# One reduction for the two norms between the blocks, the meta tokens normed early, the residual's norm on Pool

## The reference

```python
    x = ... two layers ...
    x = rms_norm(x, final_norm)                    # the residual of the second block
    h_res = concatenate([meta_tokens, x])          # 16 + 256 tokens
    h = _rmsnorm(h_res, norm_w_2)                  # what the projections read
    proj = h @ w_in_2
    ...
    return (h_res + concatenate([y_mla, y_na]) @ w_out_2)[:, 16:]
```

## Time and profile before

| | us |
|---|---|
| median of 3 runs | 1233.51 |
| the profiled execution | 1232.0 |
| its span, first to last instruction | 1230.2 |
| PE busy | 1188.6 (97%) |
| DVE busy | 815.4 (66%) |
| ACT busy | 656.6 (53%) |
| POOL busy | 165.7 (13%) |

### The profile page before, as it was taken

One profiled execution on the slowest core, in us unless ns is written; L12 is line 12 of the kernel. 1 busy time (PEld: TensorE's weight loads), 2 busy tenths in 40 slices (PEclk: granted clock), 3 DMA queues, 4 the chain that ended last, 5 costly groups with the idle time before them and its releaser, 6 DMA issues.

```text
span 1230.2 us, 27307 instructions
## 1 busy us (share of the span) xinstructions
PE 1188.6 (97%) x10002; PEld 1147.1 (93%) x10002; DVE 815.4 (66%) x1390; ACT 656.6 (53%) x1121; POOL 165.7 (13%) x228
## 2 busy tenths in 40 slices
PE   6999999999999999999999999999998989998998
PEld 6999999799999999999999899999997887998888
DVE  6767664877777665777665877777656666555764
ACT  5555543656555544555544645555545666656652
POOL 3000000351000000000000450000000000401960
PEclk9999999999999999999999999999997999999999
DMA  7655754445566744556744446556642440544542
GB/s 280 207 190 191 252 169 136 139 155 190 190 200 204 233 160 139 189 200 205 235 162 137 138 155 198 195 188 223 216 158 69 137 131 8 172 155 136 174 154 87
DMA packets 56742, 210.91 MB, mean 171 GB/s; under 512 B 7200, under 2 KB 9280, under 8 KB 56544
## 3 DMA queue, kind: packets, MB, share of 16 engines
q1 hardware_dynamic: 54048, 203.45, 50.1%
q0 software_dynamic: 2480, 6.48, 1.8%
q10 hardware_dynamic: 144, 0.06, 0.0%
HBM read 208.91 MB, written 1.05 MB: 171 GB/s over the span
## 4 chain that ended last, share of the span: by engine, by line
PE 84%; DVE 7%; ACT 3%; issue 3%; POOL 2%; DMA 0%; DVEq 0%; ACTq 0%; SPq 0%
PE bank L1173 25%; PE bank L1174 25%; PE bank L1175 25%; DVE w_lo L748 3%; PE bank L1211 2%; PE bank L1521 2%; PE bank L1501 1%; DVE h_lo L767 1%; ACT w_hi L457 1%; PE bank L1486 1%; DVE probs L886 1%; PE bank L1423 1%; PE bank L1425 1%; PE bank L1424 1%; PE bank L1481 1%
## 5 line engine op out<-in xcount | busy, mean ns | idle before, releaser
L1173 PE MATMUL bank<-h_hi,w_hi 128*128 128x256 f32 (+1 forms) x1992 | 563.4, 283 | 16.9 <-DVE w_lo L748 11.7
L1174 PE MATMUL bank<-h_lo,w_hi 128*128 128x256 f32 (+1 forms) x1992 | 554.3, 278 | 0.0
L1175 PE MATMUL bank<-h_hi,w_lo 128*128 128x256 f32 (+1 forms) x1992 | 554.2, 278 | 0.0
L748 DVE TENSOR_TENSOR w_lo<-w_raw,w_hi 128x1024 fp32r<-128x1024 f32 (+1 forms) x360 | 466.9, 1301 | 73.5 <-ACT w_hi L457 73.2
L457 ACT ACTIVATE w_hi<-w_raw 128x1024 fp32r<-128x1024 f32 (+1 forms) x360 | 397.4, 1108 | 74.4 <-PE bank L1175 56.3
L1173 PEld LDWEIGHTS bank<-h_hi,w_hi 128*128 128x128 f32 x1992 | 377.1, 189 | 24.0 <-issue 19.5
L1174 PEld LDWEIGHTS bank<-h_lo,w_hi 128*128 128x128 f32 x1992 | 377.1, 189 | 0.9
L1175 PEld LDWEIGHTS bank<-h_hi,w_lo 128*128 128x128 f32 x1992 | 376.8, 189 | 0.0
L1173 PE MATMUL bank<-g_hi,w_hi 128*128 128x256 f32 x832 | 230.8, 277 | 1.5 <-DVE g_lo L893 0.8
L1175 PE MATMUL bank<-g_hi,w_lo 128*128 128x256 f32 x832 | 230.0, 276 | 0.0
L1174 PE MATMUL bank<-g_lo,w_hi 128*128 128x256 f32 x832 | 230.0, 276 | 0.0
(11 more groups left out here) (152 smaller groups left out, 1158.6 us busy)
## 6 DMA issues: line engine op xcount, KB each, us to landing
w_raw<-in_w SPq DMA_DIRECT2D x296, 512.0 KB, 3.3
w_raw<-in_wd SPq DMA_DIRECT2D x64, 704.0 KB, 4.1
w_raw<-in_relbias POOLq DMA_DIRECT2D x64, 64.0 KB, 2.3
btab_sb<-in_btab POOLq DMA_DIRECT2D x1, 1536.0 KB, 9.5
x_res<-in_xT SPq DMA_DIRECT2D x2, 512.0 KB, 5.0
out_T<-x_res SPq DMA_DIRECT2D x8, 128.0 KB, 1.7
rope_sb<-in_rope POOLq DMA_DIRECT2D x1, 272.0 KB, 3.6
mats_sb<-in_mats POOLq DMA_DIRECT2D x1, 192.0 KB, 4.0
```

The source lines that it names most:

```text
L748: dve.tensor_tensor(wlo[:, slot, at:at + cols], raw[:, slot, 0:cols], whi[:, slot, at:at + cols].bitcast(F32), ALU.subtract).then_inc(lo_r ...
L1173: pe.matmul(o, h, xh, start=first, stop=False)
L1174: pe.matmul(o, h, xl, start=False, stop=False)
L1175: return pe.matmul(o, lo, xh, start=False, stop=last)
```

## The change

Of the final norm and the norm behind it only one reduction stays on the way to the projections. With s = sum of x² and s6 = sum of x² * (final_gain² + 1e-6), the second norm of the first norm's output is x * (final_gain * norm_w_2) * rsqrt(s6 / 1024 + 1e-12). So:

- Pool computes the gains once (`final_gains`), and in `dn2` of layer 1 adds the squares twice: plain into `acc`, weighted into `wacc` (one more multiplication and one more addition a tile).
- PE makes four sums in place of `sum_norm(6)` (`final_sums`): weighted into one bank, plain into another. The weighted one comes out first.
- ACT makes one `rstd` from the weighted sum, then the eight `h_hi`; only behind these the Ln and Exp of the plain sum, to `rs6`.
- DVE makes `h_32` at once from x by the merged gain, 256 columns wide. The three small gain multiplications and the reduction that stood between the norms now stand ahead of them.
- Pool multiplies x by `rs6` and by the gain (8 tiles, two instructions each), in place of DVE's L972; the first addition to x in `fill` waits for it.
- The meta tokens' norm is made in the first layer: Pool squares and adds (`meta_squares`, 8 x 16 columns) ahead of the convolution, PE sums 16 columns in `conv` at i == 1, ACT makes Ln and Exp at i == 2 (both in each layer, since PE, ACT and DVE loop over the layers), Pool multiplies (`meta_normed`) behind the convolution. ACT and DVE split these 8 x 16 columns at the boundary, ahead of the `rstd` (`hm_hi`, `hm_lo`).

```diff
+        g67, w6 = fin[:, 0:KT], fin[:, KT:2 * KT]
+        wacc, wsq, w6_last = s_all[:, 0:T], s_all[:, T:2 * T], pr_all[:, 0:P]
+        rs6 = rel_all[:, 0:T]
+        xm = x[:, :, T:TM]
+        msq, hm = (h32[:, i, 0:KT * META].rearrange("p (k c) -> p k c", k=KT) for i in (3, 2))
+        hm_hi, hm_lo = (a[:].rearrange("p (k c) -> p k c", k=KT)[:, :, T:TM] for a in (hhi, hlo))
...
-            def add_squares(q, n=T, tiles=range(KT - 1)):
-                for i, k in enumerate(tiles):
+            def add_squares(q, weighted=False):
+                for k in range(KT - 1):
                     pool.wait_ge(sq_done[k % 2], q * 4 + k // 2 + 1)
+                    if weighted:
+                        dst = wsq if k else wacc
+                        if k:
+                            pool.wait_ge(wsq_step, 2 * k - 1)
+                        pool.tensor_scalar(dst, sq[:, k % 2, 0:T], w6[:, k:k + 1], None, ALU.mult).then_inc(wsq_step, 1)
                     if k == 0:
-                        pool.tensor_copy(acc[:, 0:n], sq[:, 0, 0:n]).then_inc(acc_step, 1)
+                        pool.tensor_copy(acc[:, 0:T], sq[:, 0, 0:T]).then_inc(acc_step, 1)
                     else:
-                        pool.wait_ge(acc_step, q * 7 + i)
-                        pool.tensor_tensor(acc[:, 0:n], acc[:, 0:n], sq[:, k % 2, 0:n], ALU.add)\
+                        pool.wait_ge(acc_step, q * 7 + k)
+                        pool.tensor_tensor(acc[:, 0:T], acc[:, 0:T], sq[:, k % 2, 0:T], ALU.add)\
                             .then_inc(acc_step, 1)
+                    if weighted and k:
+                        pool.wait_ge(wsq_step, 2 * k)
+                        pool.tensor_tensor(wacc, wacc, wsq, ALU.add).then_inc(wsq_step, 1)
+
+            def final_gains():
+                pool.tensor_tensor(g67, sml[:, 6 * KT:7 * KT], sml[:, 7 * KT:8 * KT], ALU.mult)
+                pool.tensor_tensor(w6, sml[:, 6 * KT:7 * KT], sml[:, 6 * KT:7 * KT], ALU.mult).then_inc(fin_set, 1)
+                pool.wait_ge(fin_set, 1)
+                pool.tensor_scalar(w6, w6, EPS, None, ALU.add).then_inc(fin_set, 1)
+                pool.wait_ge(fin_set, 2)
+
+            def meta_squares():
+                pool.wait_ge(c_loaded, C_LOADS)
+                pool.tensor_tensor(msq, xm, xm, ALU.mult).then_inc(msq_step, 1)
+                for n, w in enumerate((4, 2, 1)):
+                    pool.wait_ge(msq_step, n + 1)
+                    pool.tensor_tensor(msq[:, 0:w], msq[:, 0:w], msq[:, w:2 * w], ALU.add).then_inc(msq_step, 1)
+
+            def meta_normed():
+                pool.wait_ge(ms_done, 1)
+                pool.tensor_tensor(hm, xm, rs[:, 0, T:TM].unsqueeze(1).broadcast_to([P, KT, META]), ALU.mult)\
+                    .then_inc(hm_step, 1)
+                pool.wait_ge(hm_step, 1)
+                pool.tensor_tensor(hm, hm, sml[:, 7 * KT:8 * KT].unsqueeze(2).broadcast_to([P, KT, META]), ALU.mult)\
+                    .then_inc(hm_step, 1)
...
+            final_gains()
             for l in range(LAYERS):
                 add_squares(3 * l + 1)
+                if l == 0:
+                    meta_squares()
...
                     pool.tensor_tensor(ya[:], ya[:], rs[:, 0, 0:T], ALU.mult).then_inc(y_step, 1)
+                if l == 0:
+                    meta_normed()
                 add_squares(3 * l + 2)
-                add_squares(3 * l + 3)
-            add_squares(7, TM, range(0, KT, 2))
+                if l == LAYERS - 1:
+                    pool.tensor_copy(w6_last, w6[:, KT - 1:KT].broadcast_to([P, P])).then_inc(w6_set, 1)
+                add_squares(3 * l + 3, l == LAYERS - 1)
+            pool.wait_ge(rstd_done, 8)
+            for k in range(KT):
+                pool.tensor_tensor(x[:, k, 0:T], x[:, k, 0:T], rs6, ALU.mult)\
+                    .then_inc(fx_step, 1)
+                pool.wait_ge(fx_step, k + 1)
+                pool.tensor_scalar(x[:, k, 0:T], x[:, k, 0:T], sml[:, 6 * KT + k:6 * KT + k + 1], None, ALU.mult)\
+                    .then_inc(fx_done, 1)
             pool.wait_ge(fx_done, KT)
...
-            def norm(q, n=T):
-
-                act.wait_ge(sum_done, q + 1)
-                rstd(bank[SUM][:, 0:n], 0, D, n, q + 1)
+            def final_norm():
+
+                act.wait_ge(hm_step, 2)
+                act.activation(hm_hi, hm, ACT.Copy).then_inc(hm_hi_done, 1)
+                act.wait_ge(wsum_done, 1)
+                act.activation(lnv[:, 0, 0:T], bank[SUM][:, 0:T], ACT.Ln, scale=1.0 / D, bias=EPS * EPS)\
+                   .then_inc(ln_done, 1)
+                act.wait_ge(ln_done, 7)
+                act.activation(rs[:, 0, 0:T], lnv[:, 0, 0:T], ACT.Exp, scale=-0.5).then_inc(rstd_done, 1)
                 for k in range(KT):
-                    act.wait_ge(h32_done, q * KT + k + 1)
-                    act.activation(hhi[:, k * HS:k * HS + n], h32[:, k % 4, 0:n], ACT.Copy).then_inc(h_hi, 1)
+                    high(7, k, k % 4)
+                act.wait_ge(xsum_done, 1)
+                act.activation(lnv[:, 0, 0:T], bank[XSUM][:, 0:T], ACT.Ln, scale=1.0 / D, bias=EPS)\
+                   .then_inc(ln_done, 1)
+                act.wait_ge(ln_done, 8)
+                act.activation(rs6, lnv[:, 0, 0:T], ACT.Exp, scale=-0.5).then_inc(rstd_done, 1)
...
                     if i == 2:
                         act.wait_ge(vt_done, l + 1)
+                        act.activation(lnv[:, 0, T:TM], bank[OUT][:, T:TM], ACT.Ln, scale=1.0 / D, bias=EPS)\
+                           .then_inc(ms_ln, 1)
                         act.activation(v32[:].rearrange("p t c -> p (t c)"), bank[OUT][:, 0:T], ACT.Copy)\
                            .then_inc(v_done, 1)
+                        act.wait_ge(ms_ln, l + 1)
+                        act.activation(rs[:, 0, T:TM], lnv[:, 0, T:TM], ACT.Exp, scale=-0.5).then_inc(ms_done, 1)
                     if not odd and 2 <= q < QT + 2:
...
 
-            act.wait_ge(sum_done, 7)
-            rstd(bank[SUM][:, 0:T], 0, D, T, 7)
-            act.wait_ge(c_loaded, C_LOADS)
-            for k in range(KT):
-                act.wait_ge(fx_done, k + 1)
-                if k >= 2:
-                    act.wait_ge(sq_used[1] if k % 2 else acc_step, k // 2 if k % 2 else 7 * 7 + k // 2)
-                square(k % 2, x[:, k, :])
-            norm(7, TM)
+            final_norm()
...
-            def norm(q, n=T):
-                dve.wait_ge(rstd_done, q + 1)
+            def final_norm():
+                dve.wait_ge(hm_hi_done, 1)
+                dve.tensor_tensor(hm_lo, hm, hm_hi.bitcast(F32), ALU.subtract).then_inc(hm_lo_done, 1)
+                dve.wait_ge(h_lo, 7 * KT)
+                dve.wait_ge(rstd_done, 7)
                 for k in range(KT + 1):
                     if k < KT:
-                        dve.scalar_tensor_tensor(out=h32[:, k % 4, 0:n], in0=x[:, k, 0:n],
-                                                 scalar=sml[:, bass.ds(q * KT + k, 1)], in1=rs[:, 0, 0:n],
-                                                 op0=ALU.mult, op1=ALU.mult).then_inc(h32_done, 1)
+                        dve.scalar_tensor_tensor(out=h32[:, k % 4, 0:T], in0=x[:, k, 0:T], scalar=g67[:, k:k + 1],
+                                                 in1=rs[:, 0, 0:T], op0=ALU.mult, op1=ALU.mult).then_inc(h32_done, 1)
                     if k > 0:
-                        dve.wait_ge(h_hi, q * KT + k)
-                        c = (k - 1) * HS
-                        dve.tensor_tensor(hlo[:, c:c + n], h32[:, (k - 1) % 4, 0:n], hhi[:, c:c + n].bitcast(F32),
-                                          ALU.subtract).then_inc(h_lo, 1)
+                        low(7, k - 1, (k - 1) % 4)
...
-            dve.wait_ge(rstd_done, 7)
-            for k in range(KT):
-                dve.scalar_tensor_tensor(out=x[:, k, 0:T], in0=x[:, k, 0:T], scalar=sml[:, 6 * KT + k:6 * KT + k + 1],
-                                         in1=rs[:, 0, 0:T], op0=ALU.mult, op1=ALU.mult).then_inc(fx_done, 1)
-            dve.wait_ge(fx_done, KT)
             dve.wait_ge(c_loaded, C_LOADS)
             for kind, factor in (("qn", MLA_SCALE), ("qpe", MLA_SCALE), ("naq", HD ** -0.5)):
                 gain = G_HEAD + HEAD_GAIN[kind]
                 dve.tensor_scalar(sml[:, gain:gain + 1], sml[:, gain:gain + 1], factor, None, ALU.mult)
             dve.reduce_sum(vmask[:], ident[:, P - META:P], AX_X).then_inc(second_set, 1)
-            norm(7, TM)
+            final_norm()
...
                         dve.wait_ge(w_used[piece % SLOTS], uses2(piece))
+                        if o == 0:
+                            dve.wait_ge(fx_done, KT)
                         dve.tensor_tensor(x[:, o, 0:T], fill_out(m), x[:, o, 0:T], ALU.add).then_inc(fill_taken, 1)
...
+            def final_sums():
+
+                pe.wait_ge(w6_set, 1)
+                pe.wait_ge(wsq_step, 2 * KT - 3)
+                pe.matmul(bank[SUM][:, 0:T], ones[:], wacc, start=True, stop=False)
```

(42 more changed lines are left out.)

2 lines of the change are left out of this document (1 added, 1 removed).

## The result

The change made the kernel slower: 1239.38 us (1237.52 to 1243.43, 6 runs) against 1233.3 (1232.25 to 1235.15, 6 runs), a ratio of 1.0053 [1.0039, 1.0067]. The forecast was 1222.2. The profiled execution took 1238.25, its span 1235.6, where 1218.9 was forecast.

What follows compares the result with a forecast made beforehand. PE was taken to bound the kernel, busy nearly always, with its largest loss at the boundary between blocks. Boundary gain 11.3 us, other terms 0: 1233.5 - 11.3 = 1222.2 us, range 1220.8 to 1225.0.

Steps and rivals of the forecast that it cites:

- the boundary: Between the two blocks: kpe starts at 930.05 instead of 941.36, gain 11.3 us, 8.9 removed stretch and 2.4 kv stage.
- Sums: PE's sums at the boundary: the added pair fits its idle, weighted last sum starts unchanged; cost 0, at most 0.2 us.
- ACT and DVE ahead of the first product: Boundary: hm_hi, gain instructions, reduction and hm_lo fit existing idle; cost 0 to 0.1 us on ACT, 0 to 0.15 on DVE.
- The removed stretch: Boundary: DVE's 8.88 us before h disappears; PE's first product follows h by 1.58 us, kv takes 5.95.
- The clock: PE's 2.1 us idle at the boundary: full clock taken for the forecast; a fall would cost 1.7 us.
- rival A: Clock falls at the boundary after all: PE loses 1.7 us in kv, 1223.9 us; chance 0.25.
- the comparison of 2.1 with 2.49: Argument for full clock: boundary idle of 2.1 us is shorter than the 2.49 that lowered it at the change of layers.
- The idle of 2.8 in L1366: Evidence on the clock: a later idle of 2.8 us in the trace that did not lower it.
- Pool's work on x: Behind the boundary: 16 Pool instructions, 14.6 us alone, delay DVE's w_lo but PE has margin; cost 0, bounds 0 to 2.7.
- Rival B: Behind the boundary, Pool's work on x reaches PE in part through DVE: up to 2.7 us, say 1224.2; chance 0.1.
- C: Slower than before: Pool's 16 instructions lock out DVE's splits, w_lo comes late, 14.9 us on PE, 1237.1; chance 0.02.
- The meta tokens: Mix stage: added sum, Ln, Exp and Pool instructions covered by waits, cost 0 (2.7 us uncovered); probs waits shrink or stay.

Runs made afterwards that it cites:

- e1: The changed kernel with final_gains laid into the unused h_hi_phase padding, so g and y keep their old addresses: 1226.96 us, ratio 0.994 to the kernel before.
- e2: The kernel before plus one unused 16-word tensor where the changed kernel has final_gains: 1250.36 us, ratio 1.0139.
- e3: The changed kernel with g_hi and g_lo moved back to their old place, y left 64 bytes up: 1227.17 us, ratio 0.9948 to the kernel before.
- e6: e1 without Pool's 16 instructions on x, so the second block's residual stays unnormed: 1223.09 us, ratio 0.992 to the kernel before.
- e8: e1 plus four extra sums on PE behind the fourth sum, written to a free bank: 1223.99 us, ratio 0.9924 to the kernel before.

## Why the prediction was wrong, point by point

**The step that failed is a term that is not in the sum.** The prediction gave a price to every instruction that was added, removed or moved, and none to the 64 bytes that a new tensor puts ahead of `g` and `y`: their products were left at their old rate without a word. `final_gains` was worth, in the place where it was put, 12.4 us on the changed kernel (after against e1) and 17.0 on the kernel before (e2); in the profiled spans it is 14.1 for the tiles and 2.2 for `y`. Forecast span 1218.9, plus 14.1 and 2.2, less the 2.1 at the change of layers, plus the 0.3 ahead of it, the 1.7 of the fall at 1115.7, 0.4 for the rest behind the boundary and 0.1 that the boundary gave less: 1235.6, the measured span. Most of the difference between the two prices is the clock, by the traces: one fall in the changed kernel's profiled execution, three in e1's, up to 1.7 each. Why the slower stream has fewer was not tried.

**Sums: right.** The weighted last sum starts 0.99 behind the last tile of x (933.17 - 932.18), as before (920.90 - 919.91).

**ACT and DVE ahead of the first product: right within 0.1.** `hm_lo` takes 0.28 (0.3 said), the small instructions fit before `rstd`. DVE starts on `h` 2.68 behind the last tile, 2.59 was forecast.

**The removed stretch: right.** First product 1.54 behind `h` (1.58 forecast), 4.22 behind the tile (4.2), idle 2.10 (2.1). `kv` 6.05 (5.95). `w_lo` of piece 3 starts 7.67 behind the first `h` (7.7), and no wait for it appears in PE's waits.

**The clock: the forecast held in one profiled execution, rival A in three.** Behind the same idle of 2.10 it stayed up in the changed kernel and fell in those of e1, e3 and e6, for 3.4 us each. A had a chance of 0.25 and a price of 1.7 (measured 1.56 in `kv`). These are four programs with the same work there; that one program has both outcomes, as A said, fits the mean granted clocks of e1's runs, 0.994 to 0.999 (an estimate: a fall of 3.4 us is 0.0014 of the mean, so about four falls and one), but no run shows it for this very place. (Its windows put the edges of the half clock at 467.2 and 924.6, not 467.4 and 924.7, and its four chances for "faster" add up to 0.98, not 0.97; nothing hangs on either.) The chance was too low, and the comparison of 2.1 with 2.49 was no evidence: at the change of layers the clock fell behind an idle of 1.99 (e1) and stayed up behind 2.70 (e8). The idle of 2.8 in L1366, cited as one that did no harm, did harm in the changed kernel, and in 11 of the 15 traces of this case the clock falls there: that it did not in the kernel before was luck. The changed kernel's PE timeline and a window there:
```profile
1115.82 0.90 PE L1432 MATMUL bank<-mats_sb,probs_T 128*128 128x128 f32 x3 [2.84 <-ACT probs_T L720]
...
1115.00:1120.00 5.00, 4.18 (x22) 4.18 (x23) 3.06 (x4) 3.56 (x10) 0.00 (x0) 0.66 0.72 231
```

**Pool's work on x: right.** Pool is slow beside DVE, and DVE beside Pool. Two rows of Pool's timeline in the changed kernel, then one of DVE's splits some us later:
```profile
941.56 0.74 POOL L464 TENSOR_TENSOR x_res<-x_res,rel_bias 128x256 f32<-128x256 f32 x1 [13.02 <-ACT rel_bias L547]
944.65 2.83 POOL L467 TENSOR_SCALAR x_res<-x_res,small_sb 128x256 f32<-128x256 f32 x1
```
```profile
958.62 1.83 DVE L809 TENSOR_TENSOR w_lo<-w_raw,w_hi 128x1024 fp32r<-128x1024 f32 x1
```
2.83, beside two splits of DVE, stands against 0.93 alone, 1.83 against 1.22, and the 16 instructions last 20 us, not 14.6. The Trainium skill's page "SBUF — State Buffer", section "Who interferes with whom", has a DVE instruction with two inputs in SBUF, as a split is, and a Pool instruction that reads SBUF lock each other out for a whole instruction. By that rule, the trace agrees (2.83 and 1.83). PE's margin held all the same: 0.1 to 0.5 us reach it (e6), within the bounds of 0 to 2.7. Rival B is out at its 2.0 and C at its 14.9. C was the case for "slower", and slower it was, by another mechanism.

**The meta tokens: right in e1, open by half a us in the changed kernel.** In e1 PE is 0.28 us late ahead of the mix stage of layer 0 and 0.26 behind it: the sum, Ln, Exp and Pool's instructions cost nothing. In the changed kernel, with the same instructions, the stage took 0.5 longer, and PE's first wait for `probs` there was 1.56 us, where the forecast was the 1.27 of the earlier trace rows or less; e1 had 1.11. The 64 bytes alone (e2) left it at 1.27. What made it no run shows. The changed kernel's row:
```profile
224.37 1.00 PE L1349 MATMUL bank<-mats_sb,probs 128*128 128x128 f32 x6 [1.56 <-DVE probs L946]
```

**With the bytes put right, what would the forecast have been worth?** e1 is 1226.96, 4.8 above 1222.2 and outside the range. Its profiled span is 1223.6 against 1218.9: 1.6 in `kv` at the low clock, 1.7 at 1106.3, 0.8 in the last six pieces on `y`, 0.2 ahead of the boundary, 0.1 to 0.5 by Pool. So the boundary was sized rightly, and the range was too narrow for the clock: it was drawn from the spread of three runs (1.3 us), and 25 runs of the kernel before, made later, spread from 1230.2 to 1238.9.

## What to carry to other kernels

Cost the allocations of a diff like its instructions: write down how far the weights' buffer lies from each moving operand's buffer before and after, and keep the remainder by 256 bytes, or look first whether a product in a stage that the change does not touch takes as long as before. Padding that nothing reads is part of the tuning; a small tensor belongs behind the operands or into the padding. Where a removed stall leaves an idle of some 2 us in a thin stretch, give the clock's two levels a price each, and try a few products in the gap that write to a free bank (likely worth it here, not settled). One trace in which an idle did no harm is no evidence that it does none.
